# A transformer-layer kernel's start: x host-transposed, the first modulation weights by channel tile, three weight tiles side by side

## The reference, cut to what matters

```python
mod_ctx = (silu(c_ctx) @ w_mod + b_mod)          # (9*D) for the context tokens
mod_lat = (silu(c)     @ w_mod + b_mod)          # (9*D) for the latent tokens
sh0, sc0, g0, sh1, sc1, g1, sh2, sc2, g2 = split(mod, 9)
h = rms_norm(x, n_pre[0]) * (1 + sc0) + sh0
a, b = split(h @ w_in, 2);  x = x + 0.5 * g0 * rms_norm((silu(a) * b) @ w_out, n_post[0])
```

## Time and profile before

| what | value |
|---|---|
| runs | 1794.91, 1795.15, 1797.48 us, median 1795.15 |
| profiled execution, span from first to last instruction | 1796.0 us |
| profiled execution's own total time | not listed apart from its span; the span is 0.85 us above the runs' median |
| TensorE busy | 1746.6 us, 97% of the span |
| VectorE busy | 1106.0 us, 62% |
| ScalarE busy | 726.5 us, 40% |
| share of the chain that ended last that TensorE holds | 90% |

### The profile page before, as it was taken

How to read it: one execution, slowest core, us unless ns; L and a number is a source line. 1 busy time by engine, 2 the same in 40 slices (tenths; PEclk the granted TensorE clock), 3 DMA queues, 4 the chain that set the end, 5 groups by cost and what they waited for, 6 DMA issues and landing times.

```text
span 1796.0 us, 30974 instructions
## 1 busy us (share of the span) xinstructions
PE 1746.6 (97%) x12362; PEld 1671.4 (93%) x12362; DVE 1106.0 (62%) x1968; ACT 726.5 (40%) x1310; POOL 52.8 (3%) x45
## 2 busy tenths in 40 slices
PE   6999999999999999999999999989999999999998
PEld 4999999999988999999999888889979999999997
DVE  4866566766457434555537877774458835973974
ACT  4432222212355312343454555553654433541554
POOL 0000000000020000000000000000113000000001
PEclk8999999999999999999999999999999999999999
DMA  8444444433213224323243211112412222232231
GB/s 352 140 155 141 146 138 154 147 134 118 77 42 141 71 71 94 92 87 96 78 141 117 70 39 40 39 40 71 153 62 91 72 90 72 74 107 59 92 133 59
DMA packets 53022, 183.82 MB, mean 102 GB/s; under 512 B 8593, under 2 KB 11299, under 8 KB 51875
## 3 DMA queue, kind: packets, MB, share of 16 engines
q1 hardware_dynamic: 52899, 182.10, 30.9%
HBM read 164.90 MB, written 16.52 MB: 101 GB/s over the span
## 4 chain that ended last, share of the span: by engine, by line
PE 90%; DVE 5%; ACT 2%; issue 1%; DMA 1%; SPq 0%; DVEq 0%; ACTq 0%
PE psum L649 18%; PE psum L650 17%; PE psum L651 17%; PE psum L632 4%; PE psum L633 4%; PE psum L634 4%; PE psum L689 2%; PE psum L691 2%; PE psum L690 2%; PE psum L1128 2%; PE psum L1118 2%; PE psum L1093 2%; PE psum L1008 1%; DMA mw<-in_w_mod 1%; PE psum L1176 1%
## 5 line engine op out<-in xcount | busy, mean ns | idle before, releaser
L649 PE MATMUL psum<-h_hi,whi 128*128 128x320 f32 x1520 | 478.7, 315 | 3.5 <-ACT sa L1459 3.3
L651 PE MATMUL psum<-h_hi,wlo 128*128 128x320 f32 x1520 | 470.9, 310 | 0.0
L650 PE MATMUL psum<-h_lo,whi 128*128 128x320 f32 x1520 | 470.7, 310 | 0.0
L1813 DVE TENSOR_TENSOR wlo<-raw,whi 128x1024 fp32r<-128x1024 f32 (+1 forms) x155 | 193.3, 1247 | 382.9 <-ACT whi L1223 382.9
L649 PEld LDWEIGHTS psum<-h_hi,whi 128*128 128x128 f32 x1520 | 286.1, 188 | 9.7 <-issue 5.5
L650 PEld LDWEIGHTS psum<-h_lo,whi 128*128 128x128 f32 x1520 | 286.3, 188 | 1.0
L651 PEld LDWEIGHTS psum<-h_hi,wlo 128*128 128x128 f32 x1520 | 286.1, 188 | 0.0
L1223 ACT CAST whi<-raw 128x1024 fp32r<-128x1024 f32 (+1 forms) x155 | 161.1, 1041 | 207.0 <-PE psum L651 189.8
L649 PE MATMUL psum<-g_hi,whi 128*128 128x320 f32 x512 | 158.4, 309 | 0.0
L650 PE MATMUL psum<-g_lo,whi 128*128 128x320 f32 x512 | 158.4, 309 | 0.0
L651 PE MATMUL psum<-g_hi,wlo 128*128 128x320 f32 x512 | 158.4, 309 | 0.0
(11 more groups left out here) (415 smaller groups left out, 3680.9 us busy)
## 6 DMA issues: line engine op xcount, KB each, us to landing
raw<-in_w_ffn_in SPq DMA_DIRECT2D x88, 512.0 KB, 3.6
raw<-in_w_mix SPq DMA_DIRECT2D x77, 512.0 KB, 4.1
mw<-in_w_mod SPq DMA_DIRECT2D x28, 768.0 KB, 4.9
raw<-in_w_ffn_out SPq DMA_DIRECT2D x32, 512.0 KB, 3.5
mw<-in_w_mod SPq DMA_DIRECT2D x4, 2048.0 KB, 18.1
gate<-gate_keep SPq DMA_DIRECT2D x24, 320.0 KB, 4.5
mw<-in_w_mod SPq DMA_DIRECT2D x14, 512.0 KB, 4.2
gate_keep<-gate SPq DMA_DIRECT2D x20, 320.0 KB, 4.8
```

Of the source, the lines that this page charges most:

```text
L649: mm(out, whi[t.slot][:, k, :], hi[:, k, cols], start=(k == 0), stop=False)
L650: mm(out, whi[t.slot][:, k, :], lo[:, k, cols], start=False, stop=False)
L651: last = mm(out, wlo[t.slot][:, k, :], hi[:, k, cols], start=False, stop=(k == nk - 1))
L1813: tt(lo[:, 0:nk, :], raw[t.raw][:, 0:nk, :], hi[:, 0:nk, :].bitcast(F32), ALU.subtract).then_inc(raw_free, 1)
```

## The change

- **x** arrives from the host with channels on partitions (`x_t`) and is loaded straight into x, in five pieces of 2, 2, 2, 1 and 1 channel tiles. The vectors arrive transposed too (`vec_t`). The transposes and the copies out of PSUM are gone.
- **The first modulation weights** come as eight pieces of 1 MB (`w_mod0`), one per channel tile with that tile's shift and scale columns, loaded in the order piece 0, raw 0, piece 1, raw 1, piece 2, raw 2, pieces 3 to 7, raw 3. Piece 7 shares its buffer with piece 1, so SyncE waits for `modulate(1)` before it issues it. SyncE's wait for `mod_done` is gone.
- **modulate, copy, turn, bias and scale** are done per channel tile, eight times at half or a quarter of the size. The row copies go from VectorE to ScalarE.
- **first_three** replaces `project_two`: at step s TensorE runs `modulate(s+2)`, waits for channel tile s of h, runs weight tile 0 at channel tile s, tile 1 at s-1, tile 2 at s-3, and then `turn_first(s+2)`. Tile 2 has its own weight pair `w2` and banks.
- **rows_zero** moves behind `first_three`, because its bank is now also the bank for the turned rows.
- **sum_mod(0)** and its ScalarE and VectorE parts move behind tile 4. VectorE's low part of tile 2 moves ahead into `first_normed`, so its first pass is now: multiply part 0, multiply part 1, low part of tile 3, and so on.

```diff
-            for c in range(NT):
-                src = a["x_prompt"][0] if c == 0 else a["x_sample"][0, (c - 1) * P:c * P]
-                sp.dma_start(xtok[:, c, :], src).then_inc(ld_x[c], 16)
-            for s in range(MOD_FIRST):
-                sp.dma_start(mw0[s][:, :, :].rearrange("p k c -> p (k c)"), a["w_mod"][s]).then_inc(mod0_in[s], 16)
-            for t in range(RAWS):
-                load(Tile(t), a["w_ffn_in"][t])
+            for c, (lo, hi) in enumerate(X_PARTS):
+                sp.dma_start(x[:, lo:hi, :].rearrange("p k n -> p (k n)"), a["x_t"][:, lo * N:hi * N]).then_inc(ld_x[c], 16)
+            for k in range(KC):
+                load_first(k)
+                if k < 3:
+                    load(Tile(k), a["w_ffn_in"][k])
+            load(Tile(3), a["w_ffn_in"][3])
...
-            sp.wait_ge(mod_done, 1)
...
+            def first_three():
+                for step in range(KC + LAGS[-1]):
+                    if step + 2 < KC:
+                        modulate(step + 2)
                     if step < KC:
-                        pe.wait_ge(ready, first + step + 1)
-                    for t, k in ((t0, step), (t1, step - LAG)):
+                        pe.wait_ge(h_rdy, step + 1)
+                    for u, lag in enumerate(LAGS):
+                        t, k = Tile(u), step - lag
                         if not 0 <= k < KC:
                             continue
...
+                    if step + 2 < KC:
+                        turn_first(step + 2)
...
+            def modulate(c):
+                pe.wait_ge(mod0_in[c], 16)
+                pe.wait_ge(mod0_copy, c)
                 for k in range(KC):
                     j = k % 4
-                    last = mm(psum[j * MOD_COLS:(j + 1) * MOD_COLS, ROW_BANK[s], :], silc_cols[:, k, :], mw0[s][:, k, :],
+                    last = mm(psum[j * MOD_COLS:(j + 1) * MOD_COLS, ROW_BANK, 0:2 * P], silc_cols[:, k, :], mw0[c][:, k, :],
                               start=(k < 4), stop=(k >= 4))
...
+            def turn_first(c):
+                pe.wait_ge(mod0_copy, c + 1)
...
+                    pe.wait_ge(mod_ev, c)
+                for t in range(2):
+                    last = mm(psum[:, TURN_BANK, 2 * t:2 * t + 2], mod0_rows[c % 2][:, t * P:(t + 1) * P], sel_rows[:, :],
+                              start=True, stop=True)
...
-                            project_two(Tile(base), Tile(base + 1), h_rdy, 0)
-                            tiles_in(0, 2)
+                            first_three()
+                            pe.wait_ge(pick_in, 2)
+                            pe.wait_ge(ld_cst, 16)
+                            pe.wait_ge(mod_ev, KC)
+                            mm(psum[0:MOD_ROWS, 7, :], pick_row[:, 0:MOD_ROWS], cst[:, 0:MOD_W],
+                               start=True, stop=False).then_inc(rows_zero, 1)
+                            tiles_in(0, 3, False)
+                            tiles_in(0, 0, True, 4, True)
...
+            def first_normed():
+                take_rows(0)
                 for k in range(KC):
-                    act.wait_ge(pre_t, 8 * l + k + 1)
+                    act.wait_ge(pre_t, k + 1)
+                    act.wait_ge(mod_ready, k + 1)
...
+                    copy(h_hi[:, k, :], sb[k % 2][:, :]).then_inc(pre_hi, 1)
+                    if k + 1 < KC:
+                        take_rows(k + 1)
+                    if k == 0:
+                        split(Tile(1))
+                    elif k == 1:
+                        split(Tile(2), w2[0], 0)
...
+            def first_normed():
+                times_root(0)
+                first_mod(0)
+                times_root(1)
+                for k in range(KC):
+                    dve.wait_ge(pre_hi, k + 1)
                     tt(h_lo[:, k, :], sb[k % 2][:, :], h_hi[:, k, :].bitcast(F32), ALU.subtract).then_inc(h_rdy, 1)
+                    if k + 1 < KC:
+                        first_mod(k + 1)
+                    if k == 0:
+                        split(Tile(1))
+                    elif k == 1:
+                        split(Tile(2), w2)
+                    if k + 2 < KC:
+                        times_root(k + 2)
...
+                            if late and u == 0:
+                                low_sum(0)
+                                split(t.plus(2))
                             if f == 0 and mods and u < 3:
-                                multiply(it + i, u)
+                                multiply(it + i + past // 4, u)
...
-                            elif not peeled:
+                            elif not peeled and not ((start or late) and u == 0):
                                 split(t.plus(2))
```

More of the change, by code:

```diff
@@ L51 @@
 XQ = 6
-ROW_BANK = (6, 7, 0, 1)
+ROW_BANK, TURN_BANK = 6, 7
 Y_STATS = 3
@@ L775, in turn_mod_rows, with first_stats @@
                 last.then_inc(rows_t, 1)
[L777 to L785, removed]
+            def first_stats():
+                pe.wait_ge(sq_sum, KC - 1)
+                for h in range(2):
+                    last = mm(half_out(2, h), ones_d, rb[:, HCOLS[h]], start=True, stop=True)
                 last.then_inc(ystat_mm, 1)
             pe.sem_inc(tile_done, 2)
[L789 to L799, removed]
+            pe.wait_ge(ld_small, 32)
             def first_half(l, base, u, h, ks, paced):
@@ L840, in ffn, with tiles_in @@
                 for p, nj in enumerate(PHASES):
-                    def tiles_in(i, lo=0, mods=True, past=0):
+                    def tiles_in(i, lo=0, mods=True, past=0, late=False):
                         for u in range(lo, 4):
                             project(Tile(base + past + u, i), KC, h_hi, h_lo)
+                            if late and u == 0:
+                                sum_mod(0)
                         if f == 0 and mods:
@@ L891, in _ @@
             pe.wait_ge(silc_ready, 2)
-            modulate(0)
-            modulate(1)
-            turn_first_rows(0)
-            modulate(2)
-            turn_first_rows(1)
-            stats_y(0)
-            turn_first_rows(2)
-            modulate(3)
-            turn_first_rows(3).then_inc(mod_done, 1)
-            pe.wait_ge(pick_in, 2)
-            pe.wait_ge(ld_cst, 16)
-            mm(psum[0:MOD_ROWS, 7, :], pick_row[:, 0:MOD_ROWS], cst[:, 0:MOD_W], start=True, stop=False).then_inc(rows_zero, 1)
+            first_stats()
+            for c in range(2):
+                modulate(c)
+                turn_first(c)
             ffn(0, 0)
@@ L1426, in _ @@
             fn(silc_cols[:, :, 0:2], vT[:, V_CC:V_QG].rearrange("p (g k) -> p k g", g=2), ACT.Silu).then_inc(silc_ready, 1)
-            for k in range(0, KC, 2):
-                act.wait_ge(x_t, k + 1)
-                copy(x[:, k, :], flat(0)[:, 0:N]).then_inc(x_ev[0], 1)
             act.wait_ge(eps_in, 2)
@@ L1450, in ffn, with tiles_in @@
                 for p, nj in enumerate(PHASES):
-                    def tiles_in(i, past=0, peeled=False, mods=True, last=False, entry=False):
+                    def tiles_in(i, past=0, peeled=False, mods=True, last=False, entry=False, start=False, late=False):
                         for u in range(4):
@@ L1454, in tiles_in @@
                             s = t.c // 2 % 2
+                            if late and u == 0:
+                                high_sum(0)
                             if f == 0 and mods and u == 2:
-                                high_sum(it + i)
+                                high_sum(it + i + past // 4)
                             if u % 2 == 0:
@@ L1471, in tiles_in @@
                                 prod_high(SEVEN_FROM[0] + n, 2, n, base, n)
-                            elif not peeled:
+                            elif not peeled and not (start and u == 0):
                                 split(t.plus(2))
@@ L1486, in ffn @@
                             seven(SEVEN_FROM[0] + n, n, base, SEVEN[0].start, n == SEVEN[0].stop - 1, nj)
+                    elif f == 0 and p == 0:
+                        tiles_in(0, mods=False, start=True)
+                        tiles_in(0, 4, late=True)
+                        with act.Fori(0, nj // 2 - 2) as i:
+                            tiles_in(i, 8)
                     elif f == 0 and p == 2:
@@ L2169, in ffn, with tiles_in @@
                 for p, nj in enumerate(PHASES):
-                    def tiles_in(i, mods=True, past=0, peeled=False, last=False, entry=False):
+                    def tiles_in(i, mods=True, past=0, peeled=False, last=False, entry=False, start=False, late=False):
                         for u in range(4):
@@ L2206, in tiles_in @@
                                 tt(halves(sb[s][:, :]), halves(sa[s][:, :]), both(t.bank), ALU.mult).then_inc(ev[t.slot], 1)
-                            if f == 0 and mods and u == 2:
-                                low_sum(it + i)
+                            if f == 0 and mods and not start and u == 2:
+                                low_sum(it + i + past // 4)
```

(5 more changed lines are left out.)

184 lines of the change are left out of this document (75 added, 109 removed).

## The result

The changed kernel takes 1802.47 us (median of 10 runs, 1799.33 to 1803.07); the kernel before, run beside it, took 1796.14 us (10 runs, 1793.27 to 1801.06). The ratio is **1.0033, 95% interval 1.0024 to 1.0042**: slower by 0.33%, some 6 us, where 1797.1 us and, with 60%, no change that can be told had been forecast. The profiled execution has a span of 1800.6 us, against 1796.0.

What follows compares the result with a forecast made beforehand. TensorE, busy 97% of the span, bounds the kernel: 10.5 us gained, less 1.0 `rows_zero`, 9.3 VectorE, 2.3 clock and rounding, is 1.9 us slower, 1797.1 us on the 1795.15 median. Range 1791 to 1804; the forecast's own 1793.5 to 1801.

Steps and rivals of the forecast that it cites:

- The mechanism: Ahead of tile 3: 10.5 us won in front, then lost as TensorE waits 9.3 us for VectorE's queued multiplications.
- Rival 1: Ahead of tile 3: VectorE doesn't hold TensorE, tile 3 ends 9.7 us early, 1785.5 us; chance 12%.
- 10.5 less 1.0 for `rows_zero`: Front: tiles 0 to 2 end 10.5 us earlier, at 57.7 us; `rows_zero` behind them takes 1.0 back.
- When x is summed, first turned rows: Opening: additions of squares end at 14.2 us; rows turned at 19.3 and 23.2 us.
- Rival 3: Opening: five small pieces of x arrive late by unhidden fixed costs, x 3 us later, 1800 us; chance 5%.
- The loads: After x: 10 MB at 0.43 MB per us, piece 7 landing at 34 us, wanted at 45; cost nothing.
- Rival 4: Channel steps: loads pace them, not TensorE; piece 7 landing after 45 us, at 48 us 1800; chance 3%.
- The clock in the steps: Channel steps from 23.2 us: half clock up to about 30 us, costing 3.4 us (bounds 1.7 and 21).
- Rival 2: Channel steps, 23 to 48 us: half clock lasts through; back at 38 us gives 1801, at 46 1805; chance 20%.
- What then waits: Behind `rows_zero`: TensorE idles 9.3 us for VectorE's parts 0 and 1 and low part; tile 3 starts at 68.0.
- The clock at tile 3: Tile 3 starts at 1.2 GHz after the gap, costing 2.3 us (bounds 1.7 and 3.4).
- Sum at tile 3's end: Tile 3 ends at 77.3 us, 1.9 us behind the 75.44 of before.

Runs made afterwards that it cites:

- experiments 1 to 3: Changed kernel with VectorE's first-block multiplications behind tile 3's low part and product (0.9989); with `rows_zero` ahead of step 7 (0.9978); with both, part 0 unmoved (0.9959).
- experiment 3: Changed kernel with `rows_zero` ahead of step 7 and multiply parts 1 and 2 behind tile 3's low part and the product: 1789.48 us, 0.9959 to the kernel before.
- experiment 5: Changed kernel with 21 unused products of 256 columns on TensorE between `rows_zero` and tile 3: 1800.34 us, 1.0027 to the kernel before.
- experiment 8: Both kernels profiled again, unchanged: spans of 1793.6 us (before) and 1797.5 us (after).
- experiment 6: Kernel before with only x loaded transposed in five pieces, its transposes and copies gone: 1796.43 us, 1.0002 to the kernel before.
- experiment 4: experiment 3 plus unused TensorE products, 14 ahead of the statistics and three ahead of the second turn: 1786.35 us, 0.9948 to the kernel before.
- experiment 7: Changed kernel with weight tile 2 lagging by eight channel tiles instead of three: 1801.94 us, 1.0029 to the kernel before.

## Why the prediction was right or wrong

- **The mechanism was right.** The named gap is there, with the twelve multiplications in it, ended by VectorE; experiments 1 to 3 remove it piece by piece, and nothing else comes near it in size. Rival 1 falls with it. That the change wins time in front and gives it all back was right too: experiment 3 sets it free. Its size was smaller than forecast: 7.3 us in the runs, where the prediction had 10.5 less 1.0 for `rows_zero`. Most of the difference is the base, the last but one point below.
- **When x is summed, first turned rows.** Additions end at 14.4 us (predicted 14.2), rows are turned at 19.8 (19.3) and 23.6 (23.2), the row copy takes 0.37 us (0.42). Right within half a us. The pieces of x lay over each other in the queue: each square from the third on waited for VectorE's addition, none for a load. The Trainium skill (DMA: Bandwidth & Descriptors, Bandwidth) asks for loads of 1 MiB or more; for these queued pieces of 0.33 and 0.66 MB this trace doesn't bear out that they come later. The 2 us that the prediction takes from the same page of the Trainium skill (section Anatomy of one DMA) are its fit for loads issued from GpSimd; here SyncE issues them. Rival 3 falls.
- **The loads.** No wait of TensorE for a load anywhere; 428 GB/s from 22 to 32 us. Rival 4 falls.
- **The clock in the steps.** Half clock until 32 us (taken: 30). At full clock a step takes 4.17 us (48.51 less 44.34), as 1.53 + 2.65 had it. The last rows are turned at 49.0 us, not 48.1, and so tiles 0 to 2 end at 58.7, not 57.7. Rival 2 needed 34 us and more; in the second profile the clock was back by 28 us.
- **What then waits: the step that was mis-sized.** 4.04 + 3.97 + 1.22 + 0.1 = 9.3 us was predicted, 10.2 measured. The terms that were named came to 9.4 us together, with the time between rows; the missed one is the product of tiles 0 and 1, 0.81 us (L2204): tile 3 writes into a bank that this product must have read, and the product is queued behind tile 3's low part. I had read the queue up to the weights that TensorE wants and not up to the bank it wants.
- **The clock at tile 3.** 2.3 us taken, 1.3 to 1.4 in the rows; experiment 5 agrees with it within its noise.
- **Sum at tile 3's end.** +1.0 (front), +0.9 (product), -0.9 (clock): 78.4 instead of 77.3 us, so 3.0 us behind instead of 1.9.
- **From there to the time.** Two terms that the prediction had at nothing. A fourth half-clock stretch: the changed kernel's first profile has those at 639 and 1216 us where that of the kernel before has one at 1017, which makes 1.5 us; in the second pair each has one (639 and 1017 us) and they cost the same. And the base: the profiled execution of the kernel before, on which the sum was built, had more half clock in its opening than another execution of it, 2.5 us by experiment 8. The 75.44 us that the changed kernel had to beat stood at 72.92 in the second profile. The difference at the last `sum_mod` is 3.0 us between the first two profiles, 4.2 between the second two, and 5.5 between the first of after and the second of before, which comes closest to the runs' 6. The forecast added its 1.9 us to 1795.15, the median of three times. But in the executions that list both, the time is about 2 us above the span (1802.48 and 1800.6), so the execution that the sum was built on, with its span of 1796.0, took about 1798 us. That base is 2.8 us of the 5.4 by which the forecast was low; the stretch is 1.5 and the terms up to tile 3's end are 1.1.
- **The verdict.** The forecast of no change that can be told was too mild: 1802.47 lies inside the range and beyond the forecast's own 1801. What remains open is why the clock falls at 639 us in both profiles of the changed kernel, in experiment 6 and in four others, and not in the kernel before, where the engine does the same work; the runs show that it costs 1.5 us and that it recurs, not what sets it off.

## What to carry to other kernels

When a change makes the front of a kernel faster, list for each in-order queue what stands between the new front and the first instruction that the bound engine wants next, weights and banks alike: slack that covered this work before is the first thing a faster front uses up. A signal that releases a long stretch of such work (`rows_zero` here) belongs as early as its own inputs allow, and here that one move of five lines was worth some 9 us (1802.47 to 1793.82, ratios 1.0033 to 0.9978), 7.2 of them at tile 3's start. A base that is one profiled execution carries that execution's clock; two profiles of the kernel before would have moved this forecast by more than the mis-sized terms did.

## What the runs showed of the hardware

- TensorE at 1.2 GHz for 3 us late in the run, in a stretch without idle time of its own (639 to 642 us, 14 matmuls for 22): the clock fell behind a run of 43 small transposes and matmuls, from 635.9 to 639.4 us, and did not fall behind the same run in the kernel before. Such stretches recurred at the same few places from execution to execution; one near 640, 1017 or 1216 us costs 1.5 us, the one near 540 us nothing that shows.
- Filling a wait with unused products kept the clock at 1.00 or brought it there. In front, 14 + 3 products of 256 columns gave 2 to 3 us (experiment 4); in the gap, 21 gave 1.3 us by the rows, which the runs can't tell from nothing (experiment 5). The first products ran at half clock themselves, 6 records in 2 us, and at full clock by 12 us, 11 in 2 us.
- After a gap of 10.2 us tile 3 got its full clock back after eleven matmuls, 3.0 us; after the same gap in experiment 7 it took 5.7 us. In the kernel before, the 18 matmuls in the window from 40.86 us, behind 2.5 us without work, were all at half clock, 5.4 us.
